# A streaming encoder layer: mixing and turning stages folded into the stages of the cached streams

## The chip, the cores and the metric

One Trainium2 chip, one of its cores. The kernel is one launch on that core: TensorE (PE) multiplies, VectorE (DVE), ScalarE (ACT) and GpSimd (POOL) work on vectors, SyncE (SP) issues transfers; POOL and ACT can issue transfers too, each from its own queue. The metric is device time in microseconds, the median of several executions. One further execution was profiled; rows and stage times below come from it.

## The reference, cut to what matters

One encoder layer for two request groups that share the weights: a prompt of 512 tokens and 8 decode streams of 16 tokens with 256 cached positions each, 640 tokens in all, width 1024, float32.

```python
n = rmsnorm(x, g_mix)
fq, fk, fv, ff, dq, dk, dv = split(n @ w_in)           # forgetting: 8 heads x 64; differential: 4 heads
fox_o  = softmax(fq fk^T * scale + c_q - c_k, causal) fv   # c: running sum of log-sigmoid gates
diff_o = (softmax(q1 k1^T) - lam * softmax(q2 k2^T)) dv    # rotary on dq, dk; block-causal, chunks of 64
diff_o = rmsnorm(diff_o, g_diff) * (1 - lam_init)          # per head, 128 wide
h = x + concat(fox_o, diff_o) @ w_o
mk, mv = rmsnorm(mem) @ w_mk, rmsnorm(mem) @ w_mv          # the prompt's memory; the streams' is cached
h = h + softmax((rmsnorm(h) @ w_mq) mk^T) mv @ w_mo
h = h + moe(rmsnorm(h))                                    # 4 groups x 8 experts, two experts a token
y = rmsnorm(h, g_final)                                    # new keys, values and gates are returned too
```

## The kernel before, in words

Tokens are five tiles of 128: four of the prompt, one with the eight streams. Matrices of weights and cached keys and values pass through a ring of six slots of 2 MB in a fixed order of "chunks" (`load_chunks`, L185): a chunk may be loaded once the counter `used` has passed the chunk six places ahead of it. A product of the projections runs as three matmuls on a high and a low part of both operands (`products`, L231); the parts are made slice by slice, a cast on ACT (`Split.high`, L205) and a subtraction on DVE (`Split.low`, L209), a slice being 128 rows of a chunk. The high part of a weight chunk takes a ring slot of its own.

Each stage is one `nc.Block()`: every engine has its own instruction list, the lists wait for each other by semaphores, and the next stage starts on all engines when every list of this one is through. In order, with the names that tiles of a stage begin with:

- `norm_block` (n1): normalizes and turns the input to `nT`.
- `project_block` (L478; pf for the forgetting group, pd for the differential one): queries, keys, values. Keys and values are stored by POOL; the value stores stand at the end of POOL's list (L563 to L566). TensorE's list begins with `warm_up(ps[0])`, nine transposes of the identity whose result nobody reads.
- `prompt_attention` (L722; fp, dp, mp): attention of the prompt's tokens. `warm_up(ps[5])` opens TensorE's list. For the forgetting group SP loads the causal mask here and DVE narrows mask and identity to bfloat16 (L935 to L938), for which TensorE waits. In the differential one, SP also fills the 10 MB of expert rows that no block may write with zeros (`blank`, L784 to L789) and waits for that.
- `decode_attention` (L958; fd, dd, md): the eight streams one after the other, software-pipelined: TensorE turns the cached keys of stream b + 2 (`turn_keys`), multiplies the scores of b + 1, the values of b - 1 and turns the probabilities of b (L1149 to L1154). ACT copies keys out, takes exponents and copies the turned probabilities; DVE copies keys, takes maxima, and reads the outputs out (`out`, L1208). For the differential and the memory streams each stream's output goes by four small transfers on SP to one tile of rows (L1028 to L1030), through two buffers: `out(b)` waits until the transfers of b - 2 have landed. SP loads the next chunk in the same list, behind these stores (L1031 to L1033).
- `mix_block` (L1278; m): squares, means and roots of the differential outputs, scaling, turning of the 20 pieces on TensorE, copies to `mixT` on ACT. SP loads the memory keys' weights and four small tables.
- `residual_block` (L1340; ro and rm): products with the output weights, residual sum, normalization and turning for the next stage; ro also normalizes the prompt's memory (`memN` to `mT`).
- `memory_block` (L1511; k): keys and values of the prompt's memory; `query_block` (L1593; q).
- `turn_block` (L1648; t): turns the memory streams' rows to columns, with ten more identity transposes.
- `moe_block` (L1672): routing, then blocks of 128 rows through pairs of experts, their weights in the order in which they come.

Three times, `recycle_semaphores` (L107) clears the semaphores of the finished stages behind a barrier of all engines: after fd (L2203), after the mixing stage (L2220) and after the turning stage (L2236). These two lines end TensorE's list of every decode stage:

```python
                        values(NB - 1)
                        ...
                        warm_up(ps[6], 10)
```

## Time and profile before

| | us |
|---|---|
| median of the runs shown (1358.78 to 1369.43, three runs) | 1367.72 |
| the profiled execution | 1370.57 |
| its span, first to last instruction | 1368.7 |
| busy in it: PE / DVE / ACT / POOL | 1160.4 / 450.5 / 306.0 / 81.0 |
| transferred | 326.62 MB, 239 GB/s over the span |

The stages of that execution, from the start of one to the start of the next, with the busy time of TensorE and the mean clock granted to it (1.00 is 2.4 GHz, 0.50 is 1.2 GHz):

| stage | us | PE busy | clock |
|---|---|---|---|
| n1 | 23.4 | 9.6 | 1.00 |
| pf, forgetting projection | 107.8 | 101.2 | 1.00 |
| fp, forgetting attention | 58.8 | 52.4 | 0.95 |
| fd, forgetting streams | 44.8 | 39.8 | 0.89 |
| pd, differential projection | 99.7 | 93.5 | 0.99 |
| dp, differential attention | 47.9 | 39.7 | 0.95 |
| dd, differential streams | 38.5 | 31.3 | 1.00 |
| m, mixing | 17.6 | 11.3 | 0.79 |
| ro, output projection | 78.9 | 71.4 | 0.89 |
| k, memory keys and values | 56.8 | 53.7 | 0.92 |
| q, memory queries | 65.6 | 63.1 | 1.00 |
| mp, memory attention | 40.8 | 35.0 | 1.00 |
| md, memory streams | 57.4 | 44.4 | 0.88 |
| t, turning | 3.3 | 2.0 | 1.00 |
| rm, second output projection | 77.7 | 73.7 | 0.96 |
| experts, routing included | 549.7 | 438.4 | - |

A row of the timeline gives the start, the duration, the engine, the line of the kernel, the operation, output and input with shapes, how many were merged into the row, and in brackets how long the engine had been idle and what released it. PEq, ACTq and so on are an engine's own instruction queue, SPq a transfer's issue on SP. Many small busy times are helpers' lines: L251 is `warm_up`, L207 and L212 the two halves of a split, L233 to L235 the three matmuls of a product.

### The profile page before, as it was taken

The numbers are of one execution on the slowest core, as the hardware profiler recorded it, in microseconds if no ns is written. First come the engines' busy times: TensorE is split into PE (matmuls) and PEld (weight loads), VectorE is DVE, ScalarE is ACT, GpSimd is POOL, SyncE is SP. The second block draws the span as 40 slices with busy tenths as digits, with TensorE's granted clock in tenths as the row PEclk, the third lists the DMA queues.
The fourth block names the chain that finished last, engine by engine and source line by source line (L and its number), as shares of the span: only waits on it lengthen the run. The fifth ranks groups of instructions, "written<-read, shape, count | busy, mean of one in ns | idle before, by whom it ended". The sixth has DMA issues, their size and how long they took to land. (4 is left out here: it accounts for less than half of the span.)

```text
span 1368.7 us, 17298 instructions
## 1 busy us (share of the span) xinstructions
PE 1160.4 (85%) x6654; PEld 768.5 (56%) x6655; DVE 450.5 (33%) x1017; ACT 306.0 (22%) x665; POOL 81.0 (6%) x119
## 2 busy tenths in 40 slices
PE   5998889998886999999887984999999978888870
PEld 4977556777566777799755874344444433323330
DVE  5431644531954426531444324111111100001106
ACT  7220634300634424322243310000000000000002
POOL 3110001000000000000000000000000000000003
PEclk9999989999998998999998986999999998899995
DMA  8124203124905103633155219999989999999996
GB/s 267 70 93 140 87 11 129 68 108 159 410 22 192 52 0 123 252 117 131 55 178 195 110 73 380 427 430 423 429 369 423 429 428 427 429 427 427 428 383 245
DMA packets 74686, 326.62 MB, mean 239 GB/s; under 512 B 18257, under 2 KB 20066, under 8 KB 62338
## 3 DMA queue, kind: packets, MB, share of 16 engines
q1 hardware_dynamic: 66130, 300.60, 54.8%
q0 software_dynamic: 5904, 15.77, 3.1%
q10 hardware_dynamic: 2592, 9.44, 1.7%
q8 instruction: 40, 0.66, 0.2%
q14 instruction: 20, 0.16, 0.0%
HBM read 294.52 MB, written 35.15 MB: 241 GB/s over the span
## 5 line engine op out<-in xcount | busy, mean ns | idle before, releaser
L1887 PE MATMUL bank<-ring,xT 128*64 128x512 f32 x1152 | 267.1, 621 | 39.5 <-DMA ring<-in_w 38.0
L1887 PEld LDWEIGHTS bank<-ring,xT 128*64 128x64 f32 x1152 | 97.4, 143 | 206.5 <-issue 185.6
L1904 PE MATMUL bank<-ring,hT 128*64 128x512 f32 x576 | 127.6, 595 | 16.3 <-ACT hT L1939 14.1
L2109 DVE TENSOR_TENSOR sg<-bank,sg 128x512 f32<-128x512 f32 x18 | 12.5, 692 | 283.2 <-PE bank L1887 283.2
L251 PE MATMUL bank<-ident 128*128 128x128 f32 x534 | 77.0, 310 | 30.4 <-PEq L523 10.2
L1904 PEld LDWEIGHTS bank<-ring,hT 128*64 128x64 f32 x576 | 47.6, 137 | 83.8 <-issue 83.8
L251 PEld LDWEIGHTS bank<-ident 128*128 128x128 f32 x534 | 73.3, 222 | 34.9 <-issue 34.8
L212 DVE TENSOR_TENSOR ring_r<-ring,ring_r 128x512 fp32r<-128x512 f32 x128 | 79.3, 685 | 8.8 <-ACT ring_r L207 8.6
L233 PE MATMUL bank<-ring_r,nH_r 128*128 128x512 f32 x200 | 80.5, 403 | 0.3 <-PE bank L235 0.3
L235 PE MATMUL bank<-ring_r,nT_r 128*128 128x512 f32 x200 | 79.1, 396 | 0.0
L234 PE MATMUL bank<-ring_r,nH_r 128*128 128x512 f32 x200 | 78.9, 395 | 0.0
L207 ACT CAST ring_r<-ring 128x512 fp32r<-128x512 f32 x128 | 69.1, 617 | 21.0 <-PEq L1563 15.6
L1935 ACT ACTIVATE sg<-bank 128x512 f32<-128x512 f32 x18 | 10.7, 597 | 257.5 <-PE bank L1887 257.5
L235 PE MATMUL bank<-ring_r,mixT_r 128*128 128x512 f32 x160 | 64.0, 400 | 0.0
L2114 DVE COPY yb<-bank 128x512 f32<-128x512 f32 x18 | 12.5, 692 | 132.0 <-PE bank L1904 132.0
L1939 ACT COPY hT<-bank 128x512 f32<-128x512 f32 x18 | 10.5, 585 | 179.8 <-PE bank L1895 179.8
L235 PEld LDWEIGHTS bank<-ring_r,nT_r 128*128 128x128 f32 x200 | 37.6, 188 | 9.1
L233 PEld LDWEIGHTS bank<-ring_r,nH_r 128*128 128x128 f32 x200 | 37.6, 188 | 8.8 <-issue 0.5
L234 PEld LDWEIGHTS bank<-ring_r,nH_r 128*128 128x128 f32 x200 | 37.6, 188 | 8.4
L233 PE MATMUL bank<-qnH_r,ring_r 128*128 128x320 f32 x128 | 40.5, 316 | 1.6 <-DVE ring_r L212 1.3
L1067 PE MATMUL bank<-ident,ring 128*128 128x128 f32 x256 | 36.0, 293 | 5.4 <-DMA ring<-in_cache_mem_v 2.6
L234 PE MATMUL bank<-mixT_r,ring_r 128*128 128x320 f32 x128 | 39.6, 309 | 0.0
(396 smaller groups left out, 1794.1 us busy)
## 6 DMA issues: line engine op xcount, KB each, us to landing
ring<-in_w SPq DMA_DIRECT2D x96, 2048.0 KB, 31.6
ring<-in_w_in SPq DMA_DIRECT2D x6, 2048.0 KB, 9.7
expert_rows<-dpzero SPq DMA_DIRECT2D x1, 10240.0 KB, 38.8
expert_rows<-yb ACTq DMA_DIRECT2D x18, 512.0 KB, 10.1
ring<-in_cache_mem_k SPq DMA_DIRECT2D x8, 1024.0 KB, 7.0
ring<-in_cache_mem_v SPq DMA_DIRECT2D x8, 1024.0 KB, 9.6
ring<-in_cache_fox_k SPq DMA_DIRECT2D x8, 512.0 KB, 5.2
ring<-in_cache_fox_v SPq DMA_DIRECT2D x8, 512.0 KB, 6.3
```

The lines of the kernel that those rows point to most:

```text
L207: nc.scalar.copy(r32(dst), src).then_inc(self.high_done, 1)
L212: nc.vector.tensor_tensor(r32(x), x, r32(high), ALU.subtract).then_inc(self.low_done, 1)
L233: nc.tensor.matmul(out, r32(xh), r32(yh), start=first, stop=False)
L234: nc.tensor.matmul(out, r32(xh), r32(yl), start=False, stop=False)
L235: return nc.tensor.matmul(out, r32(xl), r32(yh), start=False, stop=last)
L251: nc.tensor.matmul(bank[:, 0:P], ident[:, :], ident[:, :], start=True, stop=True)
L1067: ins = nc.tensor.transpose(bank(b, g)[:, jj * PAST + k * P:jj * PAST + (k + 1) * P], cached(b, 0)[:, k, (2 * g + jj) * P:(2 * g + jj + 1) ...
L1887: ins = nc.tensor.matmul(ps[2 + i][64 * x:64 * x + 64, :], xT[:, k, 64 * x:64 * x + 64], w(2 * i + x, t)[:, k, :], start=k == 0, stop=k == ...
L1904: ins = nc.tensor.matmul(ps[5 + half][64 * x:64 * x + 64, :], hT[:, k, 64 * x:64 * x + 64], w(4 + x, t)[:, k, half * 512:(half + 1) * 512] ...
L1935: nc.scalar.activation(sg[:, :], ps[2][:, :], ACT.Silu).then_inc(silu_done, 1)
L2109: nc.vector.tensor_tensor(hh[:, :], ps[3][:, :], sg[:, :], ALU.mult).then_inc(hid_done, 1)
L2114: nc.vector.tensor_copy(yb[:, 0:512], ps[5][:, :])
```

## The change

- The value stores of both projections are issued by ACT, behind its own work, and no longer by POOL.
- The mask is loaded with the gates' inputs and narrowed there; the forgetting attention waits for nothing of the kind. The nine identity transposes at the head of each `prompt_attention` and `decode_attention` are gone; the decode stages begin with the turning of the first keys, and DVE copies those ahead of the queries. Ten identity transposes at the end of a decode stage become six.
- SP loads chunks at the start of a decode stage, each as soon as `used` allows it; outputs are no longer stored by transfers but kept for all eight streams and turned on TensorE in the stage itself.
- `mix_block` is gone. In the differential streams ACT squares the prompt's and the streams' outputs one piece of 128 columns at a time (24 of them, with a sum each), takes roots twice (after stream 4 and at the end, with a dummy root ahead of the last streams), DVE scales, TensorE turns, ACT copies to `mixT`.
- `turn_block` is gone in the same way.
- `Ahead`: four of the eight first slices of the next stage's weights are split in the last streams (fd for pd, dd for ro, md for rm), and three slices of the query's weights and inputs in `memory_block`. The memory tile's split moves from there into ro; the small tables are loaded in `memory_block`.
- `recycle_semaphores` runs once, between ro and `memory_block`.

```diff
@@ -216,17 +218,37 @@
...
+        class Ahead:
...
+            def __init__(self, split, ch, h, at):
+                self.split, self.ch, self.h, self.at = split, ch, h, at
+                self.n = sum(len(x) for x in at.values())
...
+            def act(self, act, step):
+                for k in self.at.get(step, ()):
+                    if k == 0:
+                        wait_chunk(act, self.ch)
+                        act.wait_ge(used, self.h - SLOTS + 1)
+                    self.split.high(act, slot(self.h)[:, k, :], slot(self.ch)[:, k, :])
+            def dve(self, dve, step):
+                for k in self.at.get(step, ()):
+                    self.split.low(dve, slot(self.h)[:, k, :], slot(self.ch)[:, k, :])
...
@@ -465,6 +489,9 @@
...
+                dve.wait_ge(self.cache_in, 64)
+                nc.vector.tensor_copy(self.ident_b[:, :], ident[:, :])
+                nc.vector.tensor_copy(self.mask_b[:, :], self.mask[:, :])
...
@@ -560,10 +588,6 @@
...
-                        for i, g in enumerate(groups):
-                            if g[0] == "mm" and g[1] == "v":
-                                drained(pool, i)
-                                pool.dma_start(v_out(g[2]), vN[:, g[2], :]).then_inc(stored_v, 16)
...
@@ -664,6 +688,10 @@
...
+                        for g, grp in enumerate(groups):
+                            if grp[0] == "mm" and grp[1] == "v":
+                                drained(act, g)
+                                act.dma_start(v_out(grp[2]), vN[:, grp[2], :]).then_inc(stored_v, 16)
...
@@ -857,9 +880,6 @@
...
-                        warm_up(ps[5])
-                        if fox:
-                            pe.wait_ge(narrowed, 2)
                         for u in range(ahead * comps):
                             scores(u)
                         warm_up(ps[5], 8)
...
@@ -1020,21 +1044,9 @@
...
-                        next_chunk = chunk_range[0]
-                        for b in range(NB):
-                            sp.wait_ge(ocd, b + 1)
-                            if not fox:
-                                for h in range(4):
-                                    sp.dma_start(out_to[b * TD:(b + 1) * TD, h * W:(h + 1) * W],
-                                                 ob[32 * h:32 * h + TD, b % 2, :]).then_inc(od[b % 2], 16)
-                            if (b + 1) % streams_of_chunk == 0 and next_chunk < chunk_range[1]:
-                                load_chunks(sp, next_chunk, next_chunk + 1)
-                                next_chunk += 1
-                        assert next_chunk == chunk_range[1]
...
+                            sp.dma_start(gd[:, :], a["g_diff"].partition_broadcast(P).rearrange("p l d -> p (l d)")).then_inc(
+                                gd_in, 16)
+                        load_chunks(sp, *chunk_range)
...
-                        warm_up(ps[0])
+                        turn_keys(0)
+                        if not mem:
+                            turn_keys(1)
                         pe.wait_ge(qd, 1)
                         if not mem:
                             pe.wait_ge(qz, 2)
-                        turn_keys(0)
                         scores(0)
-                        turn_keys(1)
+                        if mem:
...
@@ -1148,14 +1176,24 @@
                                 turn_keys(b + 2)
                             if fox and b == NB - 1:
                                 out_turn(0)
+                            if mem and b == NB - 1:
+                                for g in range(3):
+                                    out_turn(g)
                             if b:
                                 values(b - 1)
                             turn(b)
+                            if diff and b >= NB - 2:
+                                for x in range(2):
+                                    out_turn(2 * (b - NB + 2) + x)
                         values(NB - 1)
-                        if fox:
-                            out_turn(1)
-                        warm_up(ps[6], 10)
+                        if diff:
+                            out_turn(TP)
+                            warm_up(ps[6], 8)
+                            out_turn(TP + 1)
+                        else:
+                            out_turn(1 if fox else 3)
+                        warm_up(ps[6], 6)
...
+                        def square(i, src):
...
+                            nc.scalar.activation(sq[:, i, :], src, ACT.Square, accum_out=ss[:, i:i + 1]).then_inc(squared, 1)
+                        def square_stream(b):
+                            act.wait_ge(ocd, b + 1)
+                            square(TP * DH + b, ob[:, b, :])
+                        def roots(i, i0, i1):
+                            act.wait_ge(mean, i)
+                            nc.scalar.activation(ss[:, i0:i1], ss[:, i0:i1], ACT.Sqrt).then_inc(root, 1)
...
                         for b in range(NB):
                             if b + 1 < NB:
                                 probabilities(b + 1)
+                            if diff and b + 2 == NB:
+                                nc.scalar.activation(idle[:, :], ident[:, 0:1], ACT.Sqrt)
                             if b + 2 < NB:
                                 keys(b + 2)
...
+                            if ahead is not None:
+                                ahead.act(act, b)
+                            if diff:
+                                if b < TP:
+                                    for h in range(DH):
+                                        square(b * DH + h, prompt[:, b, h * P:(h + 1) * P])
+                                if b:
+                                    square_stream(b - 1)
+                                if b == TP:
+                                    roots(1, 0, FIRST)
+                                if b >= NB - 2:
+                                    for x in range(2):
+                                        move(2 * (b - NB + 2) + x)
+                        if diff:
+                            square_stream(NB - 1)
+                            roots(2, FIRST, TP * DH + NB)
+                            move(TP)
+                            move(TP + 1)
...
@@ -1250,14 +1352,15 @@
                                 nc.vector.tensor_copy(qb[0:64, j, :, 0:TD], q[0:64, j])
                                 ins = nc.vector.tensor_copy(qb[64:P, j, :, TD:32], q[64:P, j])
                         ins.then_inc(qd, 1)
+                        maxima(0)
+                        keys(1)
...
+                            if diff and b == TP:
+                                means(1, 0, FIRST)
+                            if diff and b > TP:
+                                for g in ((0, 1), (2, 3), (4,))[b - TP - 1]:
+                                    normalize(g)
+                            if mem and b == NB - 1:
+                                for g in range(3):
+                                    turned(g)
...
@@ -1465,6 +1523,10 @@
...
+                            if nm and n == nm:
+                                act.wait_ge(read, nm)
+                                for k in (0, KT // 2):
+                                    mem[4].high(act, mem[3][:, k:k + KT // 2, :], mem[1][:, k:k + KT // 2, :])
...
@@ -1505,15 +1568,20 @@
...
+                            if nm and g in (6, 8):
+                                k = 2 * (g - 6)
+                                mem[4].low(dve, mem[3][:, k:k + KT // 2, :], mem[1][:, k:k + KT // 2, :])
...
@@ -1564,16 +1639,19 @@
...
-                        split.high(act, mH[:, :, :], mT[:, :, :])
                         split.high_chunk(act, W_MK, W_MK + 2)
                         split.high_chunk(act, W_MK + 1, W_MK + 3)
                         split.high_chunk(act, W_MV, W_MV + 2, free=W_MK + 1)
                         split.high_chunk(act, W_MV + 1, W_MV + 3, free=W_MK + 2)
+                        wait_chunk(act, W_MQ)
+                        act.wait_ge(used, W_MV + 1)
+                        for k in range(Q_AHEAD):
+                            q_split.high(act, nH[:, k, :], nT[:, k, :])
+                            q_split.high(act, slot(W_MQ + 2)[:, k, :], slot(W_MQ)[:, k, :])
                     @block.vector
                     def _(dve):
...
                             nc.vector.tensor_copy(dst, src).then_inc(ev, 1)
-        def query_block(nT, qT, chunk_range):
+                            if g == 7:
+                                for k in range(Q_AHEAD):
+                                    q_split.low(dve, nH[:, k, :], nT[:, k, :])
+                                    q_split.low(dve, slot(W_MQ + 2)[:, k, :], slot(W_MQ)[:, k, :])
...
@@ -2188,19 +2244,21 @@
...
+                    pd_ahead = Ahead(Split(c2, "pd"), W_DIFF, W_DIFF + 3, {b: (b - 4,) for b in range(4, NB)})
...
-                recycle_semaphores()
...
@@ -2209,34 +2267,38 @@
...
+                    ro_ahead = Ahead(Split(c1, "ro"), W_O, W_O + 2, {b: (b - 4,) for b in range(4, NB)})
+                    decode_attention("dd", "diff", qS[:, :, :], kS, vN, mixT[:, 4:8, :], C_DIFF, lamcol=lamcol,
+                                     chunk_range=(24, 26), room=spare, prompt=diffN, ahead=ro_ahead)
...
-            recycle_semaphores()
...
+                    residual_block("ro", mixT, hN, W_O, (0, 0), 1, load=x_tile, mem=(memN, mT, 2, mH, k_split), ahead=ro_ahead)
+                recycle_semaphores()
...
-            recycle_semaphores()
+                rm_ahead = Ahead(Split(c1, "rm"), W_MO, W_MO + 2, {NB - 2: (0, 1), NB - 1: (2, 3)})
+                decode_attention("md", "mem", qT[:, :, SEQ:], None, None, nT, C_MEM, chunk_range=(42, 46), ahead=rm_ahead)
```

## Rows read from the trace of the kernel before

**Rows 1.** Windows: us, PE, PEld, DVE, ACT, POOL busy, PEclk, DMA share, GB/s.

```profile
857.00:1368.70 511.70, 422.08 (x1944) 172.25 (x1944) 77.98 (x114) 30.17 (x53) 33.31 (x45) 0.94 0.97 408
```

**Rows 2.** Waits on PE, 120:138; waiter, releaser: us, times, longest.

```profile
PE bank L251 <- PEq L523: 4.7, 1, 4.7
```

**Rows 3.** Timeline, PE at the start of the differential attention.

```profile
334.58 1.84 PE L251 MATMUL bank<-ident 128*128 128x128 f32 x7 [5.45 <-PEq L523]
```

**Rows 4.** Timeline, PE at the start of the differential projection.

```profile
234.88 2.25 PE L251 MATMUL bank<-ident 128*128 128x128 f32 x18 [1.22 <-PEq L111]
```

**Rows 5.** Timeline, differential streams' end, mixing, output projection's start.

```profile
402.30 0.26 ACT L1192 COPY ddan<-bank 32x128 f32<-32x128 f32 x1 [1.18 <-PE bank L1109]
...
415.57 0.29 DVE L1213 COPY ddo<-bank 128x128 f32<-128x128 f32 x1 [2.28 <-PE bank L1124]
...
427.02 5.08 DVE L1323 SCALAR_TENSOR_TENSOR nT<-nT,mss,mgd 128x128 f32<-128x128 f32 x19
...
438.56 4.18 PE L251 MATMUL bank<-ident 128*128 128x128 f32 x18 [5.48 <-PEq L111]
```

**Rows 6.** Timeline, around the forgetting attention's start.

```profile
124.98 0.54 POOL L566 DMA_DIRECT2D out_s_fv<-fvN_  x1 [5.06 <-DVE fvN_ L634]
...
131.24 1.28 ACT L891 ACT_TABLE_LOAD   x1 [36.71 <-PEq L523]
...
136.62 0.37 ACT L891 ACTIVATE ring<-bank,fpmx 128x128 f32<-128x128 f32 x1 [4.09 <-DVE fpmx L945]
```

**Rows 7.** Timeline, memory streams, turning, second output projection's start.

```profile
710.28 3.16 PE L1067 MATMUL bank<-ident,ring 128*128 128x128 f32 x16 [2.61 <-DMA ring<-in_cache_mem_v]
...
719.43 0.86 PE L1083 MATMUL bank<-mdkt,mdqb 128*32 128x256 f32 x12
...
729.43 0.48 DVE L1215 TENSOR_SCALAR mdo<-bank,mdrs 128x256 f32<-128x256 f32 x1 [6.02 <-DMA moN<-mdo]
...
744.42 0.47 PE L233 MATMUL bank<-ring_r,rmxH_r 128*128 128x512 f32 x1 [0.78 <-DVE ring_r L212]
```

**Rows 8.** DMA issues, 120:150 and 560:580; times issued, KB each, us to landing.

```profile
out_s_fv<-fvN_ POOLq DMA_DIRECT2D x1, 256.0 KB, 5.4
...
out_p_mv<-mvN SPq DMA_DIRECT2D x1, 1024.0 KB, 4.0
```

**Rows 9.** Timeline, memory stage's end and the query stage.

```profile
571.25 0.38 SPq L131 DMA_DIRECT2D out_p_mv<-mvN  x1
571.47 2.48 DVE L1590 COPY mkT<-bank 128x512 f32<-128x512 f32 x4 [0.24 <-PE bank L1559]
...
575.01 0.82 DVE L212 TENSOR_TENSOR mixT_r<-mixT,qnH_r 128x640 fp32r<-128x640 f32 x1 [1.05 <-ACT qnH_r L207]
...
587.61 0.42 ACT L1636 ACTIVATE mqT<-bank 128x320 f32<-128x320 f32 x1
...
601.12 0.44 ACT L1636 ACTIVATE mqT<-bank 128x320 f32<-128x320 f32 x1 [6.60 <-PE bank L235]
```

**Rows 10.** Timeline, differential attention's start and end.

```profile
339.43 0.37 ACT L891 ACTIVATE nH<-bank,dpmx 128x128 f32<-128x128 f32 x1 [11.44 <-DVE dpmx L945]
...
381.45 0.69 DVE L927 COPY nT<-bank 128x512 f32<-128x512 f32 x1 [3.43 <-PE bank L851]
...
382.42 0.36 SPq L1021 DMA_DIRECT2D ddcomb<-in_c_comb  x1
```

**Rows 11.** Timeline, VectorE's splits and PE, output projection.

```profile
443.76 6.71 DVE L212 TENSOR_TENSOR ring_r<-ring,ring_r 128x512 fp32r<-128x512 f32 x11
...
452.20 1.97 PE L1415 MATMUL bank<-ident,roxs 128*128 128x128 f32 x8 [2.94 <-ACT roxs L1467]
```

**Rows 12.** Waits on SP, 320:440; the longest, and what is left behind it.

```profile
SPq L776 <- DMA expert_rows<-dpzero: 33.5, 1, 33.5
SPq L776 <- PEq L776: 2.8, 1, 2.8
```

**Rows 13.** Windows, around the differential attention's start; columns as in rows 1.

```profile
334.00:336.00 2.00, 1.42 (x7) 1.45 (x8) 0.00 (x0) 0.00 (x0) 0.96 (x1) 0.50 0.55 141
```

283 lines of the change are left out of this document (129 added, 154 removed).

## The prediction

> **What bounds the kernel now.** I read the stage table first, then the chain of waits, then each stage's seams in the timeline. The expert stage at the end keeps the DMA engines 0.97 busy for its 511.7 us [rows 1]; the diff does not touch it, so what is won ahead of it should reach the end one for one. The front is a row of blocks: each ends when its last engine is through, and all engines start the next one together. Inside the dense stages TensorE runs almost without gaps, so the gain must come from seams. They are of four kinds. (1) A block held open by a transfer: after the last value store of the first projection TensorE stands 4.7 us at the seam, after the second projection 5.45 [rows 2, 3]. (2) Start-up work that feeds nothing: nine transposes of the identity cost 2.25 us [rows 4], or 4.18 where TensorE had stood 5.48 [rows 5]; the first exponent of the forgetting attention comes 5.4 us after that stage's first instruction (136.62 against 131.24 [rows 6]). (3) Output rows carried by DMA in the memory streams, where VectorE waits 6.02 us for such stores, and TensorE 2.61 us for cached rows whose load stands behind the stores on SP [rows 7]. (4) The mixing stage: from 415.86, the end of the streams' last copy, to 438.56, the start of the next stage, there is nothing but this small stage and its waits [rows 5].
>
> **The change, step by step** (in us, against the profiled execution's span of 1368.7).
>
> *First projection's end.* The last store is issued on POOL at 124.98 and lands 5.4 later, at 130.4; the next stage starts at 131.24 [rows 6, 8]. A store that SP issued at 571.25 and that landed 4.0 later, at 575.25, did not hold its stage: VectorE's last copies end at 573.95 and the next stage is at work at 575.01 [rows 8, 9]. So POOL's queue holds a block open until its stores have landed, and SP's does not. How ScalarE's queue behaves no row shows; the bounds are nothing and the whole wait gained. I take SP's way, since both queues are listed as hardware queues and POOL's as a software one. Gain 4.7 less a bare seam of 0.3 (382.14 to 382.42 [rows 10]): **4.4**.
>
> *Forgetting attention's start.* Mask and identity are narrowed one stage earlier, in VectorE's slack, and nine transposes go. What is left ahead of the first exponent is the table load of 1.28 [rows 6]: 5.4 - 1.3 = **4.1**. If the scores were slow it would be 3.
>
> *Forgetting streams.* Nine transposes go from the head (2.25), but VectorE now copies keys (0.62, from four in 2.48 [rows 9]) ahead of the queries: 1.6. Four fewer at the tail, 0.25 each: 1.0. The clearing of semaphores goes: 1.22 idle at that seam [rows 4] against 0.3, so 0.9. Against it stand four slices of the next weights, each a cast on ScalarE and a subtraction on VectorE (0.61, from 6.71 for eleven [rows 11]). VectorE waits for the cast at the end of each stream, so the next maximum comes up to 0.7 late, four times; between 0 and 2.8 I charge 1.0, because the maximum is needed only one stream later. **2.5**. The slices save the second projection nothing: its nine transposes stay, and already cover the first splits.
>
> *Second projection's end and differential attention.* The seam (5.45 less 0.3) and the head (first exponent at 339.43, 4.85 after the start at 334.58 [rows 3, 10]; without transposes about 0.9) are worth 5.15 and 3.95. But SP ends that stage by waiting 33.5 for the transfer that blanks the expert rows, and when it has landed only 2.8 are left [rows 12]. This transfer is queued behind the loads of four chunks. The DMA engines are busy from the start on, except a dip to 0.55 over two us [rows 13], 0.9 lost. An earlier start takes away that dip with its flank, some 1.2, and no more. The stage ends 2.8 + 1.2 sooner: **4.0** of 9.1, and TensorE stands idle about 5 at its end.
>
> *Differential streams with the mixing folded in.* Before, from head to the next stage's head: 438.56 - 382.42 = 56.1 [rows 5, 10]. After: the streams took 33.4 to their last copy (415.86). The head loses 1.3. In a stream ScalarE waits 1.18 ahead of its copies [rows 5]; four or five squares of 128x128 at up to 0.37 (a 128x128 exponent [rows 10]) are 1.5 to 1.85, so three streams stretch by 0.35 each, 1.1. Square roots between exponents need the tables switched twice in the fifth stream, 2 x 1.28, of which I let 2.3 show. From the last scores on there stand in series: two tiles normalized on VectorE (8 x 0.267, from 5.08 for nineteen [rows 5]) ahead of the last maximum, 2.1; a third table load with its root, 1.5; two more tiles, 2.1; a fifth, 1.1; cast and subtraction, 1.2; statistics, 0.6; the last tile, 1.1, its turning, 0.6, and six transposes, 1.5; less 1.3 that overlap: 10.5. In sum 46.0. TensorE comes from 5 us without work and starts slow: 2.0 more. Gain 56.1 - 48.0 = **8.1**. If all of it hid, the stage would take 35 and the gain be 21; if nothing did, 0. I stay with the listing, which lies between them.
>
> Here a rule speaks against the change. By [rows 6] a table load took 1.28. The Trainium skill, "ScalarE: Activation LUTs", section "What ACT_TABLE_LOAD costs", adds a drain of about 1.38 us to every switch; by that three switches cost 4.1 more, and the sum would end 4 later.
>
> *Output projection.* TensorE waits 2.94 for the first memory tile [rows 11], which ScalarE and VectorE reach only after sixteen slices. Four slices fewer, 4 x 0.61: **2.5**.
>
> *Memory and query stages.* The clearing moves here: -0.9. The memory tile's split leaves the head: +0.7, an estimate from 0 to 4. SP issues four small loads ahead of the value weights; these are needed only half a stage later. VectorE splits three slices of the query's weights and inputs after its eighth copy, but ahead of the four copies that end the stage: 3 x (0.82 + 0.61) [rows 9, 11] = 4.3 late, while TensorE stands. The query's first group ended 13.4 after its stage's start (573.95 + 0.3 to 587.61 [rows 9]); with nine slow transposes, 4.2, a group's 7.04 (0.44 + 6.60 [rows 9]) and 1.1 of slow products it is 12.3: +1.1. **-3.4**. Were TensorE still fast, 2.25 + 7.04 would make the whole -0.4.
>
> *Memory attention.* Nine transposes go: **2.2**, between 0 and that.
>
> *Memory streams to the next projection's first product.* The head gains 1.6, as above. The 2.61 wait goes, since SP now issues a load as soon as a slot is free, and with it the slow clock behind it: sixteen transposes took 3.16, where eighteen took 2.25 [rows 4, 7], 1.2. From the last scores at 719.43 to the first product at 744.42 are 25.0 [rows 7]. After it, TensorE takes about 7 to its last values; VectorE, with two outputs, two slices and six small copies behind them, ends near 11; four last transposes and six of the identity, 12.4; the next head 2.25 if TensorE is fast, 4.2 if not. It will have waited 3 for VectorE, so I take the slow head, and 1.4 of slow products: 18.0. Gain 7.0 + 2.6 + 1.2 + 1.6 = **12.4**; 16 with a fast clock, 8 if only the two longest waits went.
>
> Sum: 4.4 + 4.1 + 2.5 + 4.0 + 8.1 + 2.5 - 3.4 + 2.2 + 12.4 = 36.8, a span of 1331.9. The profiled execution took 1370.6 with what lies around its span, 2.9 more than the median of the runs shown. On the median: 1367.7 - 36.8 = 1330.9, so **1331**.
>
> **Rivals.**
> *More comes out.* The blanking is no bound (5.1), the differential streams start fast (2.0), the query starts fast (3.0): 1331 - 10 = 1321. For it: nothing but the queue's order holds the blanking back. Against: [rows 13] leave the DMA engines 0.9 to win.
>
> *The store's wait moves along.* ScalarE's queue holds the block as POOL's did. The 4.4 are lost; after the second projection nothing more is, since the blanking binds there: 1335. For it: a store lands as late from any queue. The Trainium skill, "Trainium Kernel Development and Optimization", section "Key Constraints", says that issuing from several engines saves issue time only. By that rule alone the change of queue wins nothing here; [rows 8] show POOL's store and SP's landing after like times, but not that both are waited for.
>
> *The folded work costs what it replaced.* Table loads, 24 squares and 24 scalings stretch the differential streams to 56: 1339. ScalarE's and VectorE's slack speaks against it, TensorE's lack of it for it. If VectorE's tail takes the memory streams' gain too (12.4) and the query loses 3 more, 1355, within 1%. The drain of the page alone would give 1335.
>
> *Slower.* With 54 warming transposes gone from six heads, TensorE stays slow through the attention and stream stages. From 131.24 to 234.88 and from 334.58 to 438.56 [rows 3, 4, 5, 6] these are 208 us, with the two memory stages some 300. Nine transposes take 4.18 slow and 2.25 fast [rows 4, 5]. If a third is added, 37 cancel the gain once 110 of the 300 turn slow; all of them would give 1394. Against it: TensorE's work in a stream is the same as before.
>
> **How the numbers follow.** Forecast (1324 to 1337): 0.50. More (1315 to 1324): 0.20. The store's wait: 0.08. The drain: 0.03. The folded work: 0.12 at 1339, 0.04 at 1355. Slower: 0.03. A measurement of this kernel can tell about 1% from no change. So faster 0.93, within 1% 0.04, slower 0.03. The range holds all but the two last and the ends of the others: 1315 to 1341.
>
> **What would show it.** Right: no idle seam after either projection; a first exponent 1.4 after the forgetting attention's start; SP waiting for the blanking with nothing left behind it; three table loads in the differential streams, 44 to 50 long; VectorE splitting after the eighth copy while TensorE stands; no wait for cached rows in the memory streams. Wrong: a stage that starts only when the value stores have landed; differential streams above 52; dense stages at a low clock.

## The result, and the profile after

The changed kernel takes 1319.62 us (median of four runs, 1314.69 to 1323.8) against 1365.4 of the kernel before: ratio 0.9668, 95% interval 0.9613 to 0.9723. A second, longer comparison gave 1321.24 against 1367.1, ratio 0.9646 (0.9618 to 0.9674); this ratio leaves out one run of before, of 1548.2 us in the slower state, and is not the quotient of the two medians, which is 0.9665. So 46 us are won where 36.8 were forecast; 1320 lies in the range of 1315 to 1341, outside the likeliest case (1324 to 1337).

The two profiled spans differ by more, 1368.7 to 1312.9, which is 55.8. The table says why. Beside each kernel's first profile stands a second: for before, the stages that the kernel with eight output buffers (below) leaves unaltered; for the changed kernel, another execution of it.

| stage | before | before, second | after | after, second | gain forecast | gain measured |
|---|---|---|---|---|---|---|
| pf | 107.89 | 107.92 | 103.51 | 103.52 | 4.4 | 4.4 |
| fp | 58.74 | 57.82 | 53.64 | 53.64 | 4.1 | 4.2 to 5.1 |
| fd | 44.82 | 40.89 | 38.82 | 38.82 | 2.5 | 2.1 to 6.0 |
| pd and dp | 147.58 | 147.34 | 142.97 | 142.66 | 4.0 | 4.4 to 4.9 |
| dd and m | 56.10 | 56.12 | 45.36 | 45.40 | 8.1 | 10.7 |
| ro | 78.92 | 77.89 | 74.55 | 76.81 | 2.5 | 1.1 to 4.4 |
| k and q | 120.20 | 118.32 | 119.21 | 120.17 | -3.4 | -1.9 to 1.0 |
| mp | 42.94 | 42.93 | 40.92 | 40.92 | 2.2 | 2.0 |
| md, t and rm | 138.40 | - | 123.65 | 123.42 | 12.4 | 14.8 to 15.0 |
| experts | 549.72 | 550.49 | 547.65 | 551.41 | 0 | -1.7 to 2.8 |

The stage table ahead of the prediction sets two of its borders later than this one. By the borders used here q took 63.4 and mp 42.9 in the first profile of before (not 65.6 and 40.8), and md 56.1 and t 4.7 (not 57.4 and 3.3).

The clearing of semaphores, 0.9 of the forecast of k and q, now stands at the end of ro (TensorE idle 3.31 at that seam, 1.65 before) and is measured there.

Where code that no edit touches takes two times, the clock differs. Three windows of the kernel before (fd, ro, k) and the same three stages of its second execution (columns as in [rows 1]):

```profile
190.00:234.80 44.80, 39.79 (x430) 28.91 (x430) 16.32 (x44) 13.57 (x40) 3.35 (x12) 0.89 0.30 102
438.50:517.40 78.90, 71.35 (x314) 58.47 (x314) 33.13 (x59) 30.44 (x49) 0.00 (x0) 0.89 0.12 47
517.40:574.20 56.80, 53.74 (x226) 42.80 (x226) 29.66 (x45) 18.76 (x33) 0.00 (x0) 0.92 0.51 181
```

```profile
188.70:229.50 40.80, 35.57 (x430) 26.07 (x430) 16.37 (x44) 13.23 (x40) 3.33 (x12) 1.00 0.33 113
433.00:510.90 77.90, 70.16 (x314) 57.55 (x314) 33.14 (x59) 30.43 (x49) 0.00 (x0) 0.92 0.13 48
510.90:565.80 54.90, 51.33 (x226) 40.95 (x226) 29.67 (x45) 18.76 (x33) 0.00 (x0) 0.97 0.52 187
```

The 430, 314 and 226 matmuls are the same; at a mean clock of 1.00 instead of 0.89 the forgetting streams take 4.0 less, and the three stages together 6.8. The first profile of before was an execution with much low clock, 5 us above the median of its runs. The first profile of the changed kernel lies 5 below its median, as the fastest of four runs; its second execution took 6.5 more, 2.7 of it ahead of the experts. The expert stage, unaltered in all, took between 547.5 and 555.3 in the kernels shown here, so single times of whole kernels say nothing of 5 us here. The stage lengths say more: in the two executions of the changed kernel seven of the thirteen ahead of the experts repeat within 0.1, while the output projection differs by 2.3.

The seams after the change. End of the first projection, timeline and the last store's issue (answers to [rows 2, 6, 8]):

```profile
123.97 0.34 ACTq L694 DMA_DIRECT2D out_s_fv<-fvN_  x1
126.09 1.28 ACT L911 ACT_TABLE_LOAD   x1 [32.31 <-PEq L551]
126.13 0.46 PE L836 MATMUL bank<-fkX,fqX 128*128 128x128 f32 x2 [0.30 <-PEq L551]
127.39 0.37 ACT L911 ACTIVATE ring<-bank,fpmx 128x128 f32<-128x128 f32 x1
```

```profile
out_s_fv<-fvN_ ACTq DMA_DIRECT2D x1, 256.0 KB, 5.5
```

The store lands 5.5 after its issue, at 129.5, and the next stage has been at work since 126.1: nothing waits for it, and the first exponent comes 1.26 after the stage's start instead of 5.4.

End of the differential attention, SP's waits, and the timeline of the differential streams to the output projection's first instruction (answers to [rows 12, 5]):

```profile
SPq L801 <- DMA expert_rows<-dpzero: 34.3, 1, 34.3
...
SPq L801 <- PEq L801: 0.2, 1, 0.2
```

```profile
361.60 3.65 PE L1079 MATMUL bank<-ident,ring 128*128 128x128 f32 x16 [5.53 <-PEq L801]
...
386.24 0.22 ACT L1227 ACTIVATE ddss<-ddss 128x20 f32<-128x20 f32 x1
386.48 1.28 ACT L1214 ACT_TABLE_LOAD   x1
...
387.77 0.49 ACT L1214 ACTIVATE ddp<-bank,ddmx 128x272 f32<-128x272 f32 x1
...
388.92 0.81 PE L1095 MATMUL bank<-nH,ddqb 128*32 128x272 f32 x8 [2.23 <-issue]
...
392.75 0.44 DVE L1331 TENSOR_REDUCE ddmx<-bank 128x1 f32<-128x272 f32 x1
...
406.97 1.24 PE L273 MATMUL bank<-ident 128*128 128x128 f32 x9 [0.30 <-PEq L1037]
```

The slack of 2.8 behind the blanking is 0.2: it now ends the attention, TensorE stands 5.53 and the sixteen turns after it take 3.65, at the low clock. TensorE also stands 2.23 ahead of the last stream's scores, behind two table loads on ScalarE.

The differential streams in windows, bounded by the first, the sixth and the last of their eight maxima (columns as in [rows 1]); first the kernel before, up to its last maximum, then the changed kernel, up to the next stage:

```profile
382.42:388.20 5.78, 4.06 (x35) 3.26 (x36) 3.01 (x11) 0.58 (x1) 1.87 (x6) 1.00 0.05 12
388.20:402.79 14.59, 13.87 (x177) 9.72 (x178) 9.11 (x29) 7.67 (x23) 1.19 (x5) 1.00 0.03 7
402.79:409.27 6.48, 6.43 (x92) 4.52 (x91) 3.88 (x12) 3.45 (x11) 0.24 (x1) 1.00 0.05 13
```

```profile
361.56:366.05 4.49, 4.37 (x24) 3.48 (x24) 2.37 (x10) 0.58 (x1) 1.86 (x6) 0.57 0.18 29
366.05:380.69 14.64, 13.02 (x169) 8.90 (x170) 9.65 (x30) 11.32 (x52) 1.18 (x5) 1.00 0.01 2
380.69:392.75 12.06, 9.83 (x123) 6.63 (x123) 7.55 (x25) 9.18 (x30) 0.24 (x1) 0.86 0.03 7
392.75:406.92 14.17, 10.65 (x107) 8.61 (x106) 7.66 (x28) 8.12 (x23) 0.00 (x0) 0.88 0.71 251
```

Memory stage into query stage (answer to [rows 9]), and the end of the memory streams (answer to [rows 7]):

```profile
535.98 2.48 DVE L1668 COPY mkT<-bank 128x512 f32<-128x512 f32 x4
538.78 1.62 PE L273 MATMUL bank<-ident 128*128 128x128 f32 x6 [5.21 <-PEq L1589]
...
550.08 0.44 ACT L1715 ACTIVATE mqT<-bank 128x320 f32<-128x320 f32 x1 [1.32 <-PE bank L257]
```

```profile
674.97 0.42 DVE L1331 TENSOR_REDUCE mdmx<-bank 128x1 f32<-128x256 f32 x1 [0.88 <-PE bank L1095]
...
686.43 2.25 PE L273 MATMUL bank<-ident 128*128 128x128 f32 x18 [0.30 <-PEq L1037]
...
688.43 0.48 PE L255 MATMUL bank<-ring_r,rmxH_r 128*128 128x512 f32 x1
```

TensorE stands 5.21 while VectorE splits three slices, as forecast. From the memory streams' last maximum to the first product of the next projection it is 13.5; before it was 23.8 (720.64 to 744.42).

### The profile page after: what moved, and what is told of

Its sections match the earlier page's. It is cut to its first block and busy times, and to the rows that moved or that the text cites. A ratio compares the mean times of both kernels' runs of the same rounds, so it can differ in the third digit from the quotient of the medians.

```text
span 1312.9 us, 16868 instructions
## 1 busy us (share of the span) xinstructions
PE 1122.4 (85%) x6470; PEld 737.8 (56%) x6471; DVE 448.5 (34%) x1031; ACT 312.9 (24%) x720; POOL 76.0 (6%) x109
## 3 DMA queue, kind: packets, MB, share of 16 engines
q10 hardware_dynamic: 4032, 12.06, 2.3%
## 5 line engine op out<-in xcount | busy, mean ns | idle before, releaser
L209 ACT CAST ring_r<-ring 128x512 fp32r<-128x512 f32 x128 | 70.1, 619 | 22.0 <-PEq L1638 14.2
L1991 ACT ACTIVATE sg<-bank 128x512 f32<-128x512 f32 x18 | 10.7, 597 | 259.3 <-PE bank L1943 259.3
L273 PE MATMUL bank<-ident 128*128 128x128 f32 x338 | 48.3, 307 | 11.4 <-PEq L1589 5.2
L273 PEld LDWEIGHTS bank<-ident 128*128 128x128 f32 x338 | 46.2, 221 | 13.5 <-issue 13.4
L1995 ACT COPY hT<-bank 128x512 f32<-128x512 f32 x18 | 10.5, 585 | 177.8 <-PE bank L1951 177.8
## 6 DMA issues: line engine op xcount, KB each, us to landing
ring<-in_w_in SPq DMA_DIRECT2D x6, 2048.0 KB, 11.3
expert_rows<-yb ACTq DMA_DIRECT2D x18, 512.0 KB, 10.3
```

Of the source, the lines that this page charges most:

```text
L209: nc.scalar.copy(r32(dst), src).then_inc(self.high_done, 1)
L273: nc.tensor.matmul(bank[:, 0:P], ident[:, :], ident[:, :], start=True, stop=True)
L1995: nc.scalar.copy(hT[:, :, :], ps[4][:, :].rearrange("p (k n) -> p k n", k=ET)).then_inc(hT_ready, 1)
```

## The experiments

Each is an edit of the changed kernel, unless it says otherwise, and is read by its stage lengths.

**Value stores back on POOL.**

```diff
-                        for g, grp in enumerate(groups):
...
-                                act.dma_start(v_out(grp[2]), vN[:, grp[2], :]).then_inc(stored_v, 16)
...
+                                pool.dma_start(v_out(g[2]), vN[:, g[2], :]).then_inc(stored_v, 16)
```

> The changed kernel with the value stores back on POOL's queue, nothing else undone. Stage lengths of the changed kernel: forgetting projection 103.5 us, differential projection 94.6, differential attention 48.3. If POOL's queue holds its block open until the last store has landed and ScalarE's does not (the step as predicted), the forgetting projection takes 4.4 more, 107.9; the differential projection takes 5.1 more, 99.7, and the differential attention 4 to 5 less, since the blanking of the expert rows ends it; the differential streams then start 4.4 later in all, plus what a slow clock behind the longer seam costs in the forgetting attention (0 to 2). If the queue makes no difference (the stores' landing holds the block from either), the two projections stay at 103.5 and 94.6 and nothing moves by more than 0.5.

```profile
124.50 0.54 POOL L594 DMA_DIRECT2D out_s_fv<-fvN_  x1 [5.06 <-DVE fvN_ L662]
...
131.20 0.76 PE L836 MATMUL bank<-fkX,fqX 128*128 128x128 f32 x2 [5.11 <-PEq L551]
```

The projections took 108.33 and 99.83, 4.8 and 5.2 more; the forgetting attention 55.41, 1.8 more. So the queue decides, and not the landing: from POOL the block stays open, from ScalarE it does not. The 1.8 are what a stand of 5 costs behind itself: the same matmul of 128x128 takes 0.76 for a pair here and 0.46 without the stand; the granted clock of the stage's first seven us was 0.73 here and 1.00 there. The differential attention took 46.59, only 1.75 less; 4 to 5 had been expected. Its first loads (two chunks of the projection's own list) went out 8.4 later than in the changed kernel (318.80 against 310.43) and the stage ended 11.9 later (373.41 against 361.56), so the 5.2 of earlier start brought this end 3.5 earlier. The blanking landed 2.7 earlier; here 0.9 of other work was left behind it, so it was not quite the end of the stage.

**The wait for the blanking, one stage later.**

```diff
-                            sp.wait_ge(bd, 16)
...
                         load_chunks(sp, *chunk_range)
+                        if blanked is not None:
+                            sp.wait_ge(blanked, 16)
```

> The changed kernel, but SP waits for the blanking of the expert rows at the end of the differential streams instead of at the end of the differential attention; the transfer itself stays where it is. In the changed kernel TensorE stands 5.5 us at that seam and begins the streams at the low clock. If the blanking is the bound there (as predicted), the differential attention takes 5 less, 43.3 from 48.3, and the streams' head runs at the full clock, another 1 to 2: the output projection starts 6 to 7 sooner. Rival: the rest of the transfer goes on for 5 us beside the streams' start and their three small tables stand behind it, so VectorE waits for them and the streams take 3 to 5 more than 45.4: the output projection starts 1 to 3 sooner. If something else ended the attention, nothing moves.

The attention took 43.83, 4.5 less, so the blanking was its end. The streams took 47.94 instead of 45.4, and the output projection starts 1.9 sooner than it would have, counted from the differential projection's start (186.4 against 188.3). The rival's loss came, but not its cause: VectorE waits for no table. Timeline and the stage's first ten us:

```profile
364.39 1.13 PE L1096 MATMUL bank<-nH,ddqb 128*32 128x272 f32 x8 [1.70 <-DVE nH L1288]
```

```profile
358.80:368.80 10.00, 6.98 (x53) 5.13 (x54) 6.18 (x21) 2.81 (x7) 2.33 (x8) 0.75 0.33 121
```

TensorE, now early, stands 1.3 and 1.7 for copies of queries and keys, and the clock is low there instead. The experiment with transposes inside the waits comes back to this.

**No roots in the differential streams** (plain copies in their place; the outputs are then not normalized by them).

```diff
-                            nc.scalar.activation(ss[:, i0:i1], ss[:, i0:i1], ACT.Sqrt).then_inc(root, 1)
+                            nc.scalar.activation(ss[:, i0:i1], ss[:, i0:i1], ACT.Copy).then_inc(root, 1)
...
-                                nc.scalar.activation(idle[:, :], ident[:, 0:1], ACT.Sqrt)
+                                nc.scalar.activation(idle[:, :], ident[:, 0:1], ACT.Copy)
```

> The changed kernel with the square roots of the differential streams and the idle root ahead of the last streams replaced by plain copies of the same shape: the roots are left out, all other work stays, and with it the three loads of ScalarE's tables go from this stage. The stage takes 45.4 in the changed kernel. As predicted, 2.3 of two loads show and 1.5 of the third, so it takes about 41.5. If every switch also costs a drain of the engine beside its load, as the Trainium skill has it, three switches are worth about 8: 37 to 38. If the loads are hidden behind TensorE's and VectorE's work, it stays within 0.7 of 45.4.

The stage took 41.83, 3.5 less. From the sixth maximum to the last, and from there to the next stage:

```profile
382.52:393.32 10.80, 9.12 (x126) 6.13 (x126) 7.45 (x24) 6.62 (x28) 0.24 (x1) 1.00 0.09 18
393.32:405.06 11.74, 9.04 (x102) 7.16 (x102) 7.56 (x28) 6.83 (x22) 0.00 (x0) 1.00 0.75 273
```

The first of the two is 1.3 shorter than with two loads of 1.28; the second is 2.4 shorter than with one, but there the clock is also 1.00 instead of 0.88. If the third load shows in full, the loads make about 2.5 of the 3.5, and the rest goes with the clock. Nothing beyond the loads' own 3.84 is seen. The output projection took 77.19, 0.4 to 2.6 more: the load that it found done before now stands in its path, and its first memory tile comes 11.4 after its start instead of 10.9:

```profile
413.55 1.28 ACT L1518 ACT_TABLE_LOAD   x1
...
416.47 1.97 PE L1470 MATMUL bank<-ident,roxs 128*128 128x128 f32 x8 [3.52 <-ACT roxs L1525]
```

**The query's slices earlier.**

```diff
-                            if g == 7:
-                                for k in range(Q_AHEAD):
+                            if g in (5, 6):
+                                for k in ((0, 1), (2,))[g - 5]:
```

> The changed kernel with VectorE's three splits of the query's weights and inputs moved from behind its eighth copy of the memory stage to behind the sixth (two slices) and the seventh (one), where it waits 4.9 us for TensorE each time. The memory stage takes 57.3 and the query stage 61.9 in the changed kernel; TensorE stands 5.2 between them and begins the query stage at the low clock. If the splits stand in the way of the four last copies (as predicted, 4.3), the memory stage takes 52.9 to 53.3, and the query stage begins at the full clock, 1.5 to 2 less: together 5.5 to 6.5 less. Rival: ScalarE's casts of these slices come too late for the earlier place, VectorE's seventh copy waits for them, and the two stages together change by less than 1.5.

```profile
535.17 0.69 DVE L1668 COPY mvN<-bank 128x512 f32<-128x512 f32 x1 [3.57 <-PE bank L257]
...
538.90 1.35 PE L273 MATMUL bank<-ident 128*128 128x128 f32 x10 [1.53 <-PEq L1589]
```

53.73 and 59.97: 3.5 and 2.0 less, 5.5 in all. VectorE still waits 3.57 ahead of its eighth copy, so the slices there were free, and the stand of 5.21 is 1.53.

**The kernel before, with eight output buffers** in the differential and memory streams.

```diff
-                obs = NB if fox else 2
+                obs = NB
...
-                            if b >= 2 and not fox:
-                                dve.wait_ge(od[b % 2], 16 * 4 * (b // 2))
```

> The kernel before with eight output buffers instead of two in the differential and the memory streams, so that no output waits for a store; the stores themselves, the order of SP's list, the mixing and the turning stage stay. In the kernel before the memory streams took 56.1 us and VectorE waited 7.8 in them for the stores of its two buffers, 6.0 at the last but one and 1.8 at the one ahead of it. If those waits carry the end of the streams (as predicted), the memory streams take 5 to 7 less, about 50; the 2.6 wait for cached rows, whose loads stand behind stores on SP, stays. Rival: SP still issues the last stores one after the other and waits for their landing, so the end comes as late as before, within 2 us of 56.1, and the gain of the changed kernel there is that of turning without transfers. The differential streams, where no such wait showed, stay at 38.5 in both.

The differential streams stayed at 38.5. Memory streams and turning stage took 52.23 and 6.81, together 59.04 against 60.77. The rival holds for the two stages together: VectorE's last output is done at 717.97, but the turning starts at 724.39, when SP has got the last stores through:

```profile
717.49 0.48 DVE L1213 TENSOR_SCALAR mdo<-bank,mdrs 128x256 f32<-128x256 f32 x1 [1.34 <-PE bank L1120]
...
719.45 3.12 SPq L1029 DMA_DIRECT2D moN<-mdo  x5
...
724.39 1.94 PE L1654 MATMUL bank<-ident,moN 128*128 128x128 f32 x8 [4.54 <-PEq L1013]
```

The second projection took 79.9 instead of 77.6, at a granted clock of 0.93 instead of 0.96, so that nothing of the 1.7 reached the experts. So the 6.02 of [rows 7] was no gain by itself; removing the transfers was.

**No slices ahead** in the three stream stages.

```diff
...
-                    pd_ahead = Ahead(Split(c2, "pd"), W_DIFF, W_DIFF + 3, {b: (b - 4,) for b in range(4, NB)})
+                    pd_ahead = Ahead(Split(c2, "pd"), W_DIFF, W_DIFF + 3, {})
...
```

> The changed kernel without the four slices of the next weights in the forgetting, the differential and the memory streams; those of the query stay. Stage lengths of the changed kernel: forgetting streams 38.8 to 40.4 (over five runs), differential projection 94.6, differential streams 45.4 to 46.8, output projection 74.6 to 75.8, memory streams 44.8, second output projection 78.9. As predicted, the forgetting streams take 1 less and the differential projection the same; the differential streams 1.2 less and the output projection 2.5 more; the memory streams about 1.5 less and the second projection 0 to 2 more: in sum within 2 of the changed kernel. Rival: the slices pace the first group of each following stage as they did in the query stage, where three slices took about 4 from its first group; then the two output projections take 3 to 5 more each and the whole is 5 to 9 slower. The other rival: the slices only cost, and the whole is 3 to 4 faster.

Forgetting streams 39.91 and differential projection 94.57: no change. Differential streams 41.21, 4.2 less, and output projection 78.73, 1.9 to 4.2 more. Memory streams 41.52, 2.9 to 3.3 less, and second projection 79.32, 0.3 to 0.5 more. The experts start at 764.91 against 765.25 and 767.99, although the input stage took 1.1 more here: the slices bring nothing on balance, and in the memory streams they cost 2.6 to 2.8. In the differential streams, from the sixth maximum to the last and from there to the next stage:

```profile
383.02:392.88 9.86, 8.15 (x121) 5.68 (x122) 6.25 (x22) 8.13 (x28) 0.24 (x1) 1.00 0.01 2
392.88:404.72 11.84, 9.35 (x108) 7.66 (x108) 6.46 (x26) 7.08 (x21) 0.00 (x0) 1.00 0.78 280
```

They take 2.2 and 2.3 less than with slices. The second of the two is in part the clock (1.00 instead of 0.88); the first is not, for with slices it takes 12.06 at 0.86 and at 1.00 alike (the second experiment ran it at 1.00). In the output projection the slices do what was forecast: the first memory tile comes 10.9 after the stage's start with them and 13.3 without, 13.7 in the kernel before. The changed kernel and this one, wait for that tile:

```profile
417.85 1.09 PE L1470 MATMUL bank<-ident,roxs 128*128 128x128 f32 x8 [3.04 <-ACT roxs L1525]
```

```profile
PE bank L1470 <- ACT roxs L1523: 4.8, 1, 4.8
```

**The identity transposes back** at the head of the six attention and stream stages.

```diff
+                        warm_up(ps[5])
                         for u in range(ahead * comps):
...
+                        warm_up(ps[0])
                         turn_keys(0)
```

> The changed kernel with the nine identity transposes back at the head of each of the six attention and stream stages. By the prediction they are start-up work that feeds nothing: each costs 2.25 at the full and 4.2 at the low clock where nothing else is waited for, so the forgetting and the memory attention take about 2 more each (53.6 and 40.9), the streams 1 to 2 more (38.8 to 40.4, 45.4 to 46.8, 44.8), the differential attention nothing, since the blanking ends it: 6 to 10 in sum. Rival (the low clock): the transposes keep TensorE's clock up through the heads of the streams, where the records show it at 0.5 in the forgetting streams (some 6.8 us) and in the differential streams (6.8); if they do, those low stretches go, and the streams take the same or up to 2 less than without.

Forgetting attention 55.66, memory attention 42.93 (2.0 more each), differential attention 48.64 (0.3 to 0.6), streams 42.27, 48.58 and 48.25 (1.9 to 3.5, 1.8 to 3.2 and 3.1 to 3.8 more). In sum some 13, more than expected, and the clock gained nothing: over the first ten us of the forgetting and the differential streams it was 0.91 and 0.83, against 0.91 and 0.81 without them. In the differential streams the transposes ran at the low clock themselves, behind the stand that the blanking leaves.

```profile
367.59 3.87 PE L273 MATMUL bank<-ident 128*128 128x128 f32 x18 [3.83 <-PEq L801]
```

**Blanking, slices, and transposes inside the waits.** The edits of the second and fourth experiment, and thirteen identity transposes where TensorE waits for copies at the head of the differential streams.

```diff
...
+                            warm_up(ps[6], 6)
                         pe.wait_ge(qd, 1)
...
                         scores(0)
...
+                            warm_up(ps[6], 7)
...
```

> The changed kernel with three edits: SP waits for the blanking at the end of the differential streams; the query's slices stand behind the sixth and seventh copy; and TensorE makes thirteen identity transposes where it waits for copies at the head of the differential streams. Where the blanking alone was moved, the differential attention took 4.5 less, but TensorE stood about 3 in the streams' head, the clock fell to 0.5 there, and the streams took 47.9 instead of 45.4. If the clock explains that, the transposes keep it up and the streams take 45 or less: the output projection starts 5 sooner than in the changed kernel (401.9), and with the slices' 5.5 the memory attention starts about 10 sooner. If the streams' loss has another cause (their small tables behind the blanking), they stay at 47 to 48.

```profile
358.00:368.00 10.00, 9.78 (x93) 7.74 (x96) 7.09 (x23) 4.40 (x18) 2.63 (x9) 1.00 0.36 134
```

The streams took 44.97 instead of 47.94, with the clock at 1.00 where it was 0.75; the attention 43.87, memory and query stage 53.73 and 59.97. The memory attention starts at 592.53, 8.2 sooner than in the first profile of the changed kernel though the input stage took 1.1 more. From the first to the sixth maximum the streams took 14.65 here at a clock of 1.00, and 17.36 in the second experiment at 0.80: 2.7 of the 3.0 between the two. So the loss of the second experiment went with the clock. That the transposes kept the clock up is not shown. With the value stores back on POOL the same stands are there without any transpose, and the clock stayed at 1.00 (timeline and first ten us of that run's differential streams):

```profile
373.46 1.94 PE L1079 MATMUL bank<-ident,ring 128*128 128x128 f32 x16 [1.05 <-PEq L801]
376.72 0.67 PE L1095 MATMUL bank<-nH,ddqb 128*32 128x272 f32 x8 [1.32 <-DVE ddqb L1353]
379.08 0.67 PE L1095 MATMUL bank<-nH,ddqb 128*32 128x272 f32 x8 [1.70 <-DVE nH L1287]
```

```profile
373.45:383.45 10.00, 6.97 (x74) 4.92 (x78) 7.29 (x23) 4.61 (x18) 2.61 (x9) 1.00 0.06 15
```

One execution of each kernel does not settle it.

**The changed kernel again.**

> The changed kernel once more, unaltered, for its stage lengths in a second execution and for its time beside the next kernel. If the prediction's sum fell short because the profiled execution of before was one with much low clock (in the kernel with eight output buffers the unaltered forgetting streams took 40.9 instead of 44.8, the output projection 77.9 instead of 78.9 and the memory stage 54.9 instead of 56.8: 6.8 us together), then the changed kernel's stages ahead of the experts agree within 3 us with those of its first profile (765.2 at the experts' start), and its median lies 43 to 48 below that of before, 10 less than the 55.8 between the two profiled spans. If the 55.8 are the change's own, its median lies 52 to 58 below.

The experts start at 767.99 (765.25 in the first profile), and the median lies 45.9 below that of before. That is the first of the two outcomes: 10 of the 55.8 belong to the two executions that were profiled, about half to each.

**All that paid.** The kernel of the experiment "Blanking, slices, and transposes inside the waits", with the transposes also in the forgetting streams, no slices in the memory streams, and the idle root behind the copies of its stream.

```diff
...
-                rm_ahead = Ahead(Split(c1, "rm"), W_MO, W_MO + 2, {NB - 2: (0, 1), NB - 1: (2, 3)})
+                rm_ahead = Ahead(Split(c1, "rm"), W_MO, W_MO + 2, {})
```

> The changed kernel with the wait for the blanking at the end of the differential streams, the query's slices behind the sixth and seventh copy, thirteen identity transposes in the waits at the head of the forgetting and the differential streams, no slices of the second output projection in the memory streams, and the idle root behind the copies of its stream. From the earlier runs: attention 4.5, memory and query stage 5.5, memory streams 2.8; if the late root lets TensorE's 2.5 wait in the seventh stream shrink to about 1, the differential streams take 43.5 instead of 45.0; if the transposes hold the clock in the forgetting streams too, these take 37 to 38 instead of 38.8 to 40.4. The experts then start at 750 to 753 instead of 765, and the median lies 12 to 15 below that of the changed kernel. If the two new edits do nothing, 754 to 756 and 9 to 11.

1304.25 us (1302.08 to 1306.49), ratio 0.9534 to before (0.9506 to 0.9562), 17 less than the changed kernel in the same comparison (1321.24). That is more than the 12 to 15 expected, for another reason than the two new edits: the experts start at 754.87, 10.4 and 13.1 sooner than in the two executions of the changed kernel, and the expert stage, which no edit touches, took 3.8 less than in the second of them (547.6 against 551.4). Memory streams 41.54; the late root brought nothing (44.80). With the transposes the forgetting streams took 38.41 at a clock of 1.00; without them they took 38.8 to 40.4 at 0.91 to 0.96.

## Why the prediction was right, and where it was not

**First projection's end: right, step and size.** 4.4, and 4.8 when undone. That ScalarE's queue behaves as SP's was a choice between bounds; the store's row (landing at 129.5, next stage at 126.1) settles it. By the Trainium skill, "Trainium Kernel Development and Optimization", section "Key Constraints", taken alone, the change of queue would have won nothing; what was won is not issue time but the block's end, on which that rule does not bear.

**Forgetting attention's start: right.** 5.4 became 1.26. Of the gain, 2.0 is the transposes (put back, they cost that).

**Forgetting streams: not to be judged to the us.** Unaltered code took 40.9 and 44.8 before, the changed 38.8 to 40.4 in the kernels that leave them alone. The claim that the slices save the second projection nothing held (94.57 without them, 94.63 with); the 1.0 charged for them did not show.

**Second projection's end and differential attention: right.** 4.0 forecast, 4.4 to 4.9 measured; 2.6 of it is the slack of the blanking (2.8 had been put), and 2.0 its earlier landing, counted from the projection's start (1.2). The blanking took the rest of the seam's gain back, and TensorE stands 5.53 at the end ("about 5"). The case "more comes out" named this, the streams' fast start and the query's fast start as its mechanisms. None of the three happened (5.53, 3.65 for sixteen turns, 5.21), although the time falls in that case's bracket: its number is right by luck.

**Differential streams: mechanism right, two charges that did not come due.** To the first maximum 5.8 became 4.5, the 1.3 that were forecast. The slow start lies in this stretch (clock 0.57); where the clock is 1.00 it takes 4.0 (second experiment, and with transposes in the waits). So the 2.0 charged for it on top were 0.45. From the first to the sixth maximum, with 15 of the 24 squares, 14.59 became 14.64: the stretch of 1.1 did not come either. From the sixth to the last, 6.5 became 12.1, 5.6 more. This stretch takes 12.06 at a clock of 0.86 and at 1.00 (second experiment), so the clock has no part in it; by the experiments 1.3 are two table loads (2.3 forecast) and 2.2 the slices. That leaves 2.1, which is what the two tiles normalized ahead of the last maximum had been put at. From the last maximum to the next stage the forecast was 6.6 (the old streams' way to their last copy) and 8.4 of its 10.5 in series, 15.0; it took 14.2, at a clock of 0.88. Against the sum the head is 2.0 shorter, the first five streams 1.1 and the end 0.8, and the stretch between 1.2 longer, since the slices cost more than the 1.2 put for a cast and a subtraction (4.2 in all by the experiment, part of it clock). From the drain that the Trainium skill adds to every switch ("ScalarE: Activation LUTs", section "What ACT_TABLE_LOAD costs") an estimate for three switches is 4.1 more than their loads. This case does not show it: without them the stage is 3.5 shorter, less than the three loads' own 3.84, and in the rows above the load begins 0.02 after the root ahead of it has ended and the exponent 0.01 after the load.

**Output projection: right step and size, but not by a shorter wait.** The first memory tile was to come 2.5 sooner; it comes 10.9 after the stage's start instead of 13.7, and 13.3 without the slices. TensorE's wait for it stays at 3.0 all the same, because TensorE too is there sooner: its first product comes 2.05 after the start (408.97 from 406.92) instead of 3.87, and the clock of the stage's first eight us is 1.00 instead of 0.62. From that tile to the stage's end two executions of one kernel differ as much as the two kernels (63.6 and 65.9 in the changed one, 64.2 and 65.2 before), so the whole gain can only be put between 1.1 and 4.4.

**Memory and query stages: too dark.** Without the clearing the forecast was -2.5; measured was -1.9 to 1.0. The slices do stand in the way (3.5 of the 4.3, by the experiment), and the query starts slow. What the step undervalued is what they give: the first group is done 11.3 after the stage's start instead of 13.4, forecast 12.3, and the memory stage's first product comes 1.3 sooner, where 0.7 was put.

**Memory streams: right way, too small.** Head 2.4 (forecast 1.6), middle 4.3 (3.8), tail 10.3 (7.0). In the tail the step that failed is the head of the second projection: it was charged 4.2 and 1.4 for a slow clock, and ran at the full one (2.25). TensorE waits for no load in these streams any more (0.4 in the second execution), as forecast. From its first product to its end the second projection took 76.8 instead of 74.6. That is the clock again, and not the change: the kernel before with eight buffers took 76.8 too, and both ran at 0.93 over the stage where the first profile of before ran at 0.96. Of the stores' waits the forecast had counted the 6.02 as if it carried the end; the eight buffers show that taking it away alone wins 1.7.

**Memory attention: right.** 2.0 of the 2.2 forecast, and put back the transposes cost 2.0.

**The sum.** Against typical executions the forecast is 9 too small, spread over the differential streams (2.6), the memory streams (2.5), memory and query (about 2) and less in the others. The common mark: most parts held a charge for something late or slow, and several of these did not come due (the slices in the forgetting streams, the slow start and the stretch of the differential ones, the slow head of the second projection). The profiled execution of before held 7 us of low clock more than another one of the same code; the sum priced none of that, which was right for the median and would have looked wrong beside the two spans. One sum of the last rival is wrong: all 300 us slow are 100 more, which on 1331 gives 1431 and not 1394; nothing else rests on it.

## What to carry to other kernels

Look at what a block waits for before its work: a store's queue, or a wait for a transfer that nothing in the next stage reads, can hold all engines. Splitting the next weights early pays only where the engine that splits would otherwise stand (behind the sixth copy, not behind the eighth; not in the memory streams). Profile unaltered stages twice before taking a term of 3 us from one execution.

## What the hardware showed that was not expected

- Low clock was seen behind stands, but not behind every one: with the blanking as bound TensorE stood 5.53 and ran at 0.81 on average over the next 10 us; with that stand gone, stands of 1.05, 1.3 and 1.7 were followed by 0.75 in one run and by 1.00 in another. With transposes in the waits it was 1.00.
- Transposes ahead of the work, where nothing else is waited for, kept no clock up and cost 1.8 to 3.8 a stage (0.3 to 0.6 where the blanking ends it). With transposes in the waits the differential streams took 3.0 less than in the run at 0.75; how much of that is theirs is open.
- The same 430 matmuls of a stage took 40.8 and 44.8 us in two executions, at mean clocks of 1.00 and 0.89.
